# Two attentions of a hybrid mixer, heads taken in pairs, with the scores on row halves of the array and retention's values on column halves

## What is computed

```python
# mLSTM, per head
sc = jnp.einsum('bhid,bhjd->bhij', qc, kc) * w        # w = exp(log_w - m_row), causal
num = jnp.einsum('bhij,bhje->bhie', sc, vc) + ...     # den = row sums of sc + ...
hc = num / jnp.maximum(jnp.abs(den), jnp.exp(-m_row))[..., None]
# retention, per head, after rope on q and k
sc = jnp.einsum('bhid,bhjd->bhij', qc, kc) * intra    # intra: powers of a per-head decay, causal
o = jnp.einsum('bhij,bhje->bhie', sc, vc) + ...
```

## Time and profile before

| | us |
|---|---|
| median of three runs | 3358.9 (3358.81 to 3363.27) |
| the profiled execution | 3359.39 |
| its span in the profile | 3357.5 |
| PE busy | 3289.8 (98%) |
| DVE busy | 1725.5 (51%) |
| ACT busy | 1271.2 (38%) |
| POOL busy | 30.5 (1%) |
| the attentions of layer one lie in | about 422 to 560 us |
| those of layer two in | about 1522 to 1665 us |

### The profile page before, as it was taken

One profiled execution on the slowest core, in us unless ns is written; L12 is line 12 of the kernel. 1 busy time (PEld: TensorE's weight loads), 2 busy tenths in 40 slices (PEclk: granted clock), 3 DMA queues, 4 the chain that ended last, 5 costly groups with the idle time before them and its releaser, 6 DMA issues.

```text
span 3357.5 us, 38789 instructions
## 1 busy us (share of the span) xinstructions
PE 3289.8 (98%) x15294; PEld 2688.4 (80%) x15294; DVE 1725.5 (51%) x2424; ACT 1271.2 (38%) x1870; POOL 30.5 (1%) x62
## 2 busy tenths in 40 slices
PE   8999999999999999999999999999999999999998
PEld 7888876788888888887668888877888888888887
DVE  4443455765443444345575544455556577454433
ACT  4222334443222322233444332335454467332321
POOL 0000000000000000000000000000000000000000
PEclk9999999999999999999999999999999999999999
DMA  4233321113233232322211322321211233333231
GB/s 150 96 98 92 104 75 59 38 57 104 97 95 97 96 99 93 99 92 82 65 42 42 111 96 94 96 87 57 69 57 61 84 93 96 105 99 98 97 93 65
DMA packets 107396, 288.05 MB, mean 86 GB/s; under 512 B 22912, under 2 KB 34176, under 8 KB 107216
## 3 DMA queue, kind: packets, MB, share of 16 engines
q1 hardware_dynamic: 91696, 278.70, 26.1%
q10 hardware_dynamic: 14208, 2.63, 0.4%
q0 software_dynamic: 1312, 4.25, 0.4%
HBM read 282.64 MB, written 2.88 MB: 85 GB/s over the span
## 4 chain that ended last, share of the span: by engine, by line
PE 89%; DVE 6%; ACT 3%; issue 1%; ACTq 1%; DMA 1%; DVEq 0%; SPq 0%
PE ps L785 27%; PE ps L787 26%; PE ps L786 26%; PE ps L794 2%; DVE mf L2150 1%; DVE wl L1964 1%; PE ps L1101 1%; PE ps L1257 1%; PE ps L1096 1%; ACT wh L1370 1%; PE ps L1239 1%; ACT L1361 1%; PE ps L799 1%; PE ps L1253 0%; ACTq L1662 0%
## 5 line engine op out<-in xcount | busy, mean ns | idle before, releaser
L1370 ACT ACTIVATE wh<-raw 128x1024 fp32r<-128x1024 f32 (+3 forms) x581 | 567.3, 977 | 1680.3 <-PE ps L787 1647.4
L785 PE MATMUL ps<-hnh,wh 128*128 128x512 f32 x2712 | 1080.6, 398 | 2.9 <-DVE hnl L1979 2.0
L787 PE MATMUL ps<-hnh,wl 128*128 128x512 f32 x2712 | 1060.8, 391 | 0.0
L786 PE MATMUL ps<-hnl,wh 128*128 128x512 f32 x2712 | 1060.1, 391 | 0.0
L1964 DVE TENSOR_TENSOR wl<-raw,wh 128x1024 fp32r<-128x1024 f32 (+3 forms) x581 | 652.1, 1123 | 591.3 <-ACT wh L1370 588.1
L785 PEld LDWEIGHTS ps<-hnh,wh 128*128 128x128 f32 x2712 | 512.2, 189 | 123.9 <-issue 19.6
L787 PEld LDWEIGHTS ps<-hnh,wl 128*128 128x128 f32 x2712 | 511.4, 189 | 108.6
L786 PEld LDWEIGHTS ps<-hnl,wh 128*128 128x128 f32 x2712 | 512.5, 189 | 106.7 <-issue 3.4
L785 PE MATMUL ps<-mr,wh 128*128 128x512 f32 x1300 | 509.2, 392 | 2.8 <-DVE mr L2626 2.0
L787 PE MATMUL ps<-mr,wl 128*128 128x512 f32 x1300 | 506.1, 389 | 0.0
L786 PE MATMUL ps<-mr,wh 128*128 128x512 f32 x1300 | 505.9, 389 | 0.0
(11 more groups left out here) (293 smaller groups left out, 2407.4 us busy)
## 6 DMA issues: line engine op xcount, KB each, us to landing
raw<-in_w_in SPq DMA_DIRECT2D x140, 512.0 KB, 3.5
raw<-in_ffn_w_gate SPq DMA_DIRECT2D x88, 512.0 KB, 3.5
raw<-in_ffn_w_up SPq DMA_DIRECT2D x88, 512.0 KB, 3.5
raw<-in_ffn_w_down SPq DMA_DIRECT2D x64, 512.0 KB, 3.5
raw<-in_w_ffn_in SPq DMA_DIRECT2D x44, 512.0 KB, 3.5
raw<-in_ffn_w_down SPq DMA_DIRECT2D x32, 384.0 KB, 3.0
raw<-in_w_out SPq DMA_DIRECT2D x32, 256.0 KB, 2.6
raw<-in_w_out_ssm SPq DMA_DIRECT2D x32, 256.0 KB, 2.6
```

What stands on the lines that cost most here:

```text
L785: self.e.matmul(out, ah, bh, start=start, stop=False, skip_group_check=shared)
L786: self.e.matmul(out, ah, bl, start=False, stop=False, skip_group_check=shared)
L787: m = self.e.matmul(out, al, bh, start=False, stop=stop, skip_group_check=shared)
L1370: self.e.activation(k.spl[u % NSPL][0][:, 0:n], k.raw[u % NRAW][:, 0:n], ACT.Copy).then_inc(k.w_hi, 1)
```

## The change

Both attentions take two heads, a pair, at a time.

- **Scores.** `scores` issues for each key block jt the two heads' matmuls one behind the other: head one from partitions 0 to 63, head two from 64 to 127, each into a bank of its own (`SCORE_AT`). Blocks 0, 1 and 3 stand together; block 2, whose banks are those of block 0, comes at a later step, behind the weighing of block 0.
- **mLSTM** of pair p: spread at steps 0 and 2 (the second behind the first head's `dm`, since both use one bank), `dm` at 1 and 3, exponentials at 2 and 4, scores at 4 and 9, weighing of both heads at 6, 7, 8 and 11, values at 13 and 16, unchanged in shape. A pair comes every 16 steps, as before, but the first spread of pair two stands at step 16 and its scores at step 20. `mlstm_pair`: spread of the bound at 5, maximum 6, squares 7, sum matmul 9, sum 10, root 12, result 14.
- **Retention** of pair p, a pair every 9 steps from step 42: scores at 0 and 5, weighing at 2, 3, 4 and 7, values at 10. The values are now eight matmuls of 64 output columns: head one's results go to PSUM partitions 0 to 63, head two's to 64 to 127 of the same bank, and ACT copies all 128 rows at once. Squares at 12, their matmul at 14, root at 15, result at 17.
- Both heads' weights need a second set of slots (`R_D`, `M_D` are pairs), and the four tables of decays get four slots, so GpSimd loads all of them ahead. The delta rule's queries, keys and values change slots (`of_head`), the first convolution of its values waits for the sums of squares, and some of GpSimd's fills move.
- `PACE_ATT` 0.98 becomes 1.05, `ATT_STEPS` 65 becomes 70, `AT_RET` 40 becomes 42.

```diff
-PACE_ROWS, PACE_ATT, PACE_BOTH, PACE_DELTA = 1.1, 0.98, 2.0, 1.3
+PACE_ROWS, PACE_ATT, PACE_BOTH, PACE_DELTA = 1.1, 1.05, 2.0, 1.3
...
+SCORE_AT = ((((6, 0), (2, 0)), ((7, 0), (3, 0)), ((6, 0), (2, 0)), ((7, 384), (3, 384))))
...
-ATT_STEPS, AT_ROPE, AT_RET = 65, 34, 40
+ATT_STEPS, AT_ROPE, AT_RET, PER_PAIR, PER_RET = 70, 34, 42, 16, 9
...
+    def scores(self, q, kk, p, jt, ups):
+
+        k, w = self.k, T - 128 * jt
+        for s in range(2):
+            (bank, at), pr = SCORE_AT[jt][s], slice(64 * s, 64 * s + 64)
+            m = self.e.matmul(k.ps[bank][:, at:at + w], k.slot(kk + p)[pr, 128 * jt:128 * jt + 128], k.slot(q + p)[pr, 128 * jt:T],
+                              start=True, stop=True, skip_group_check=True)
...
+        if s in (0, 2):
             self.wait_ge(k.row_v, 5 * l + 2)
             self.wait_ge(*k.rows_v.at(l, "acol"))
...
+            if s:
+                self.wait_ge(*V.at(n, "dm0"))
+            elif p:
+                self.wait_ge(*V.at(n - 1, "dm1"))
+            self.spread(k.slot(M_NG, dt=R), 2 * p + s // 2, B_PAIR, P.up(n, f"sp{s // 2}"))
+        if s == 4:
+            if p:
+                self.wait_ge(*V.at(n - 1, "t2"))
             self.wait_ge(k.took, self.qk_took[2 * l])
...
+            self.scores(M_Q, M_K, p, 0, up("s0", "t0"))
+            self.scores(M_Q, M_K, p, 1, None)
+            self.scores(M_Q, M_K, p, 3, up("s3", "t3"))
+        if s == 9:
+            self.wait_ge(*V.at(n, "t0"))
+            self.scores(M_Q, M_K, p, 2, up("s2", "t2"))
...
             for jt in range(4):
...
+                for i in range(2):
+                    at = 128 * (2 * p + i) + 64 * i
+                    m = self.e.matmul(k.ps[B_ATT][64 * i:64 * i + 64, 128 * jt:T], k.slot(R_V + jt)[:, at:at + 64],
+                                      k.slot(R_D[i], 3)[:, OFF[jt]:OFF[jt] + T - 128 * jt], start=jt == 0, stop=jt == 3,
+                                      skip_group_check=True)
             m.then_inc(*P.up(n, "v"))
...
+            self.e.activation(k.slot(R_Q + p)[:, :], k.ps[B_ATT][:, :], ACT.Copy).then_inc(*k.rh_a.up(n, "num"))
```

More of the change, by code:

```diff
@@ L280, in blk, with of_head @@
     return t[:, :].rearrange("p (c n) -> p c n", c=4)
+def of_head(kind, h):
+    return M_QKV + 4 * kind + h
 def wide(t):
@@ L517, in mixer @@
         parts = [k.pair(D_PART + 2 * i, D_PART + 2 * i + 1) for i in range(4)]
-        parts += [k.pair(M_QKV + 3 * h, M_QKV + 3 * h + 1) for h in range(4)]
+        parts += [k.pair(of_head(0, h), of_head(1, h)) for h in range(4)]
         first = self.out_first(l, y, parts)
@@ L536, in attention @@
         for t in range(ATT_STEPS):
[L537 to L541, removed]
-            self.rope(l, t - AT_ROPE)
[L543 to L547, removed]
+            for p in range(2):
+                self.mlstm(l, p, t - PER_PAIR * p)
+            for p in range(2):
+                self.mlstm_pair(l, p, t - PER_PAIR * (p + 1))
+            self.rope(l, t - AT_ROPE)
+            for p in range(2):
+                self.retention(l, p, t - AT_RET - PER_RET * p)
+                self.retention_pair(l, p, t - AT_RET - PER_RET * p)
             yield
@@ L1091, in delta @@
         yield
-    def score(self, q, kk, h, jt, up):
-        k = self.k
-        p, pr, w = h // 2, slice(64 * (h % 2), 64 * (h % 2) + 64), T - 128 * jt
-        self.e.matmul(k.ps[B_SCORE[jt]][:, 0:w], k.slot(kk + p)[pr, 128 * jt:128 * jt + 128], k.slot(q + p)[pr, 128 * jt:T],
-                      start=True, stop=True).then_inc(*up)
-    def values(self, v, d, h, jt):
-        k = self.k
-        return self.e.matmul(k.ps[B_ATT][:, 128 * jt:T], k.slot(v + jt)[:, 128 * h:128 * h + 128],
-                             k.slot(d, 3)[:, OFF[jt]:OFF[jt] + T - 128 * jt], start=jt == 0, stop=jt == 3)
@@ L1106, in mlstm @@
+    def mlstm(self, l, p, s):
+        k, n = self.k, 2 * l + p
         P, A, V = k.mh_p, k.mh_a, k.mh_v
-        if h >= 4:
-            return
-        n = 4 * l + h
-        if s == 0:
+        up = lambda *names: [lambda name=name: P.up(n, name) for name in names]
+        if s in (0, 2):
             self.wait_ge(k.row_v, 5 * l + 2)
             self.wait_ge(*k.rows_v.at(l, "acol"))
-            if h:
-                self.wait_ge(*V.at(n - 1, "w3"))
-            if h == 3:
-                self.wait_ge(*k.mp_v.at(2 * l, "sum"))
-            self.spread(k.slot(M_NG, dt=R), h, B_PAIR, P.up(n, "sp"))
-            self.wait_ge(k.took, self.qk_took[2 * l])
-            for jt in range(4):
-                self.score(M_Q, M_K, h, jt, P.up(n, f"s{jt}"))
@@ new lines, in mlstm @@
+        if s in (13, 16):
+            i = (s - 13) // 3
+            self.wait_ge(k.took, self.v_took[2 * l])
+            if i or p:
+                self.wait_ge(*(A.at(n, "abs0") if i else A.at(n - 1, "abs1")))
+            self.wait_ge(*V.at(n, ("s2", "t2")[i]))
+            for jt in range(4):
+                h = 2 * p + i
+                m = self.e.matmul(k.ps[B_ATT][:, 128 * jt:T], k.slot(M_V + jt)[:, 128 * h:128 * h + 128],
+                                  k.slot(M_D[i], 3)[:, OFF[jt]:OFF[jt] + T - 128 * jt], start=jt == 0, stop=jt == 3)
+            m.then_inc(*P.up(n, f"v{i}"))
@@ L1175, in retention_pair @@
         k, n = self.k, 2 * l + p
-        if s == 12:
+        if s == 14:
             self.wait_ge(*k.rp_a.at(n, "sq"))
```

228 lines of the change are left out of this document (109 added, 119 removed).

## The result

| | before | after |
|---|---|---|
| median (7 runs each) | 3360.8 us (3358.8 to 3363.3) | 3351.3 us (3349.6 to 3355.9) |
| profiled execution, span | 3359.39, 3357.5 us | 3352.85, 3351.0 us |

The ratio is 0.9976, with a 95% interval of 0.9967 to 0.9986: some 8 us faster, a little over what a measurement of this kernel can tell. The forecast was 3350.5. So the number was right, but the traces show that two of its parts were wrong and cancelled.

What follows compares the result with a forecast made beforehand. TensorE, busy 98% of the span, was taken as the bound. Overlap -18.9, turning +3.5, waits +5.3 and clock +1.7 sum to -8.4 from 3359.4, giving 3351.0, stated as a 3350.5 us median; range 3342 to 3366.

Steps and rivals of the forecast that it cites:

- Side by side: Paired scores and retention's values in both attentions: two heads' matmuls overlap on array halves, saving 12.0 + 6.9 = 18.9 us.
- head two lags head one by one record: Paired bursts: head two's records run beside head one's, one record later; a pair's scores take 2.80 us, retention's values 2.58.
- The signs named for the burst: Scores of blocks 0, 1 and 3, between neighbouring products: 2.6 to 2.8 us; 3.4 or more without overlap, 1.7 without lag.
- Turning: Switching the array's form around attention bursts: 0.41 us per 64-row stretch, 0.35 per column-half stretch, together +3.5 us.
- Waits: TensorE's waits in both layers' attentions: 13.2 us before, 18.5 after, so +5.3, bounds -1 and +10.
- The single blocks' waits: TensorE's waits at values for single blocks' weighing, 4.6 us over both layers, go to nearly nothing.
- Clock: Around attention waits TensorE's granted clock falls to 0.50; five or six stretches lose 8.5 us against 6.8, so +1.7.
- Rival four: Overlap as forecast, but four wait places each 1 us longer and three more half-clock stretches: 3360 us, chance 0.12.
- products outside 422 to 560 and 1522 to 1665 us change their time: Sign that the prediction is wrong: product matmuls outside these time windows change their time.
- Rival one: Paired scores and values overlap fully, no lag at all: 25.8 us saved in place of 18.9, 3343.6 us, chance 0.12.
- Rivals two and three: Two: no overlap, slower, 3369.4 us, chance 0.14. Three: row halves overlap, column halves don't, 3357.4 us, chance 0.08.

Runs made afterwards that it cites:

- The two runs in turn: Changed kernel with head one's matmuls all issued before head two's: scores of blocks 0, 1 and 3, 3362.6 us; retention's values, 3358.0 us.
- the changed kernel with the second block as before: Changed kernel with one added line setting the side-work counter to 0.8 at the second block's start: 3343.2 us, ratio 0.9949.
- The one profile with the counter set: Changed kernel with the side-work counter set to 0.8 and 0.2 at the delta stages, 0.6 at layer two's attentions, 0.8 at the second block: 3341.3 us.
- Two programs whose orders are alike up to the second block: Changed kernel with both attentions' sum matmuls three steps later, 3339.8 us; the same with the counter set to 0.8 at the second block, 3337.9 us.

## Why the prediction was right, and where it wasn't

- **Side by side**: the direction was right and the size wrong. The failed step is "head two lags head one by one record", 18.9 us. No record lags; it is 25.8. I took records of the queue to start strictly in turn because they do so in the rows that I read, and said that no row of before could test the other; but the trace of before has four places where neighbours use different row halves, and they start 3 ns apart. The two runs in turn show that the order matters, though less strictly than I had it. The signs named for the burst were 2.6 to 2.8 us between neighbouring products and 1.7 with no lag; from the last product ahead to the first behind it is 2.25 (431.04 - 428.79) with no lag, since turning the array is in it.
- **Turning**: 0.42 for rows and 0.36 for columns, predicted 0.41 and 0.35, both as what is left of a burst once full overlap is taken out.
- **Waits**: 8.4 at L992 (predicted 8.95), 6.3 at L1153 (6.35), 3.2 at L1195 (3.2), 1.0 elsewhere (0): 18.9 against 18.5. Following each engine's queue with durations of before gave these to within 0.5 us. The single blocks' waits of 4.6 us went as said.
- **Clock**: six stretches and 8.7 us lost in the first profile, four and 6.6 in the second of the same kernel; predicted five or six and 8.5. So this term is good to some 2 us at best. Rival four, with longer waits and three more stretches, came in neither.
- **The second block**: not in the sum at all, and it cost 7.6 us. I had read the order only around the attentions. The prediction names "products outside 422 to 560 and 1522 to 1665 us change their time" as a sign that it is wrong, and that sign came. The unforeseen loss and the undersized gain (6.9) cancel, and that is why 3350.5 was so near to 3351.3: luck. With the right overlap and nothing else changed the sum would have been 3343.6, and the changed kernel with the second block as before, which takes the loss away, measured 3343.2.
- Rival one was the true mechanism, at a chance of 0.12. Rivals two and three fell with the first burst on row halves and on column halves.

Layer one's delta stage was not in the sum either. Taken whole it is 3.2 and 1.3 us longer in the changed kernel's two profiles, and layer two's is 1.3 and 1.6 shorter. The one profile with the counter set has both as before to within 0.1 us. What stays open is why the stretches at half clock fall where they do, and with them 2 to 3 us of each layer.

## To carry to other kernels

Where a program interleaves side work by a running counter, a changed pace, or a changed number of steps, moves every later instruction: compare the order of the whole program, also where no line was edited, or reset the counter at each stage. Two float32 matmuls of 64 rows, or of 64 output columns, cost what one costs if they stand next to each other in the queue, plus some 0.4 us for turning the array there and back; with all of one head ahead of all of the other, less than half of the saving is left. Before taking such an overlap from a model, look in the trace at hand for neighbours that already use different halves. When a change gets near its forecast, compare stretch by stretch before believing the reasons.

## What the runs showed of the hardware

- Neighbouring matmuls on the two row halves or the two column halves start 7 ns apart, with both records of each: two cost what one does. When all of head one stands ahead of head two, 0.77 of 1.72 us (rows) and 0.60 of 2.15 us (columns) still overlap. In both, head two's first record starts when three of head one's, ahead of it in the queue, haven't started.
- A stretch of 64 rows between products costs 0.41 us beyond its columns, of 64 columns 0.36, of four columns 0.30.
- The kernel before, profiled twice, has its half-clock stretches at the same places to within 0.1 us. The changed kernel, profiled twice, has not: in layer one's attentions they start at 468.2, 509.2 and 546.7 us (13.6 us together) in one profile, at 511.4 and 545.6 (6.8) in the other. Two programs whose orders are alike up to the second block (about 2170 us) had six and ten of its 3.4 us pieces before that. The changed kernel's layer one differs by 3.4 us between its two profiles, half of it in the attentions. So a difference of 2 to 4 us between two kernels of this size can come without any edit.
